# A one-layer hybrid encoder with 32 experts: the branch for crowded experts moved ahead of the last expert, and small loads put on shared semaphores

## The chip, the core and the metric

The kernel runs on one core of a Trainium2 chip. The time is that of one execution on the device in microseconds (us), as a median of several runs. The core has a matrix engine (TensorE, in the profile PE, its weight loads PEld), VectorE (DVE), ScalarE (ACT), GpSimd (POOL) and SyncE (SP). Each engine runs its own instruction stream in order, and the streams meet only at semaphores. Data moves between memory and the core by 16 DMA engines.

## What is computed

One layer on a sequence of 256 tokens of width 1024, all in float32. A mixing part (attention and a state-space branch) comes first. Then each token goes to its 4 best of 32 experts, and at the end an embedding term is added through a gate:

```
logits = hf @ w_router + b_router            # 256 x 32
top_val, top_idx = top_k(logits, 4);  gate = softmax(top_val)
# for every expert e, on the rows (tokens) that chose it:
gu  = xb @ w_up[e] + b_up[e]                  # 1024 -> 2048
g   = minimum(gu[:, :1024], 7);  up = clip(gu[:, 1024:], -7, 7)
act = (up + 1) * g * sigmoid(1.702 * g)
y   = act @ w_down[e] + b_down[e]             # 1024 -> 1024
x  += sum over the 4 experts of gate * y
# at the end
x  += sigmoid(rmsnorm(x, g_ple_gate) @ w_ple_gate) * rmsnorm(p @ w_ple_proj, g_ple_post)
```

An expert's weights are 12 MB (8 MB up, 4 MB down). Nothing bounds how many of the 256 tokens choose one expert. With these inputs no expert has over 64.

## The kernel before

**Pieces and ring.** An expert is six pieces of 2 MB: pieces 0 to 3 are the up weights, 4 and 5 the down weights. They go through a ring of 9 places in SBUF (`ring`). SP issues the loads (`load_pair`, `load_piece`, DMA at L410 and, in two halves, L477). Ahead of each it waits until the piece that lay in the place before has been read (`left`, L467 and L469): PE counts up a semaphore when it has read a piece (`READ`, `.then_inc`). Behind the pieces of the 32 experts come two pieces of the gate's weights (L503).

**One expert on PE.** `up` (L1638) waits for pieces 0 to 3 in turn and multiplies the tokens that chose the expert, at most `CAP` = 64 of them, by the up weights into banks `UG` and `UU`. `gather` (L1612) collects the next expert's tokens. `down` waits for the activation, transposes it (L1676), transposes the selection (L1680), multiplies by pieces 4 and 5 (L1694), adds the next expert's bias into `UG` and `UU` (`up_bias`, L1514), and scatters the result to the tokens (L1712). DVE clamps and multiplies (L1154 to L1162) and adds the scattered result to the residual (L1180). ACT does the sigmoid (L761) and two copies (L763, L765).

**Order of the experts.** PE has experts 0 to 2 and 27 to 31 written out, and those between in a loop of three experts a turn. ACT and DVE loop over one expert a turn. Within expert 12 the embedding product and the bias of the down product are done beside the rest (`embeddings`, L1739 and L1749, `bias_too`, L1710).

**The last expert** (31, `n == E - 1`) is written out apart on PE and DVE, in ACT it is the last turn of its loop. Its piece 3 and piece 5 come in two halves. PE turns the residual ahead (`turn_ahead`, L1653) into the banks `XT3B` and adds the last expert's share on top there (`scatter_turned`, L1662); DVE (L1170) and ACT (L782) copy the sum to `XT3`. Then come the gate's products (`gate`, L1817, 80 records), ACT's squares (L794), root (L796) and sigmoids (L800), DVE's products and sums (L813, L1259), and five stores by SP (L517).

**The branch for crowded experts.** DVE writes the largest count of tokens of an expert to `flag` early (`flag_set`). Each of PE, ACT, DVE and SP loads `flag` into a register (`value_load`) and, where it is over 64, runs loops over all experts and three further passes of 64 tokens each, on semaphores `M` that go on counting. This branch stands behind expert 31: on PE at L1790 between expert 31's scatter and the gate, on DVE at L1231, on ACT at L785, on SP at L507 behind the gate's loads. With these inputs it isn't taken, and each engine jumps over its body.

Of the kernel before, what the change touches and what calls it, by code (L numbers as in the profile page):

```python
# [68 lines left out]
def hybrid_layer(nc, x, p, g_mix, w_in, g_q, g_k, w_attn, a_re, a_im, log_dt, b_re, b_im, c_re, c_im, d_skip,  # L69
# [19 lines left out]
    with ExitStack() as ctx:  # L89
# [34 lines left out]
        def spread(ap, n):  # L124
# [47 lines left out]
                 for at in (6, 7)]  # L172
# [67 lines left out]
        names = ("x_in_0 x_in_1 half_in gain_mix_in params_in later_in dt_in bc_in ident_set odd_set b_zero x_sq x_ms x_root x_normal dt_rows angle_set "  # L240
                 "sine_set turn_set bbar_set pool_tables_set head_sq head_ms head_ms_all head_root heads_set "
                 "abs_set soft_set sp_set cum_full early_gates_set back_set gelu_set sz_set mixed_set x_again "
                 "x2_sq x2_ms x2_root x2_normal xn_set xn_half w_sum m_sum prod_full prod_read router_in router_set slots_set top_set exp_set chosen_set sel_first_set "
                 "gx_half xs_half cnt_full flag_set gates_ready "
                 "down_bias_in gain_in gate_gain_in cast_set cast_first_set rest_set_0 rest_set_1 up_bias_in up_bias_set post_in ple_in pp_ms pp_root "
                 "pt_full pt_set pp_full pp_set gt_full gt_set over_done late_0 late_1 late_2 xt3_late xt3_again xt3_read xt3_again_set x3_set x3_sq x3_ms x3_root xt3_full xt3_set pg_full "
# [3 lines left out]
                     "at_set y_full y_set sc_full sc_add dve_step").split()  # L250
        M = {n: sem("e_" + n) for n in moe_names}

# [12 lines left out]
        READ = {c: sem(f"read{c}") for c in (0, 1, 2, 4)} | {3: M["up_u"], 5: M["y_full"]}  # L265
# [30 lines left out]
        OVER = [spot(E - 1, c) for c in range(PER_EXPERT)]  # L296

# [94 lines left out]
        def _(sp):  # L392
# [20 lines left out]
            for key in W_ORDER:  # L413
# [14 lines left out]
                if key == ("attn", 0):  # L428

                    sp.dma_start(GFFN.rearrange("p (c k) -> p c k", k=4),  # L430
                                 g_ffn[0].rearrange("(c p k) -> p c k", p=P, k=4)).then_inc(S["gain_in"], 16)
                    sp.dma_start(GROUT.rearrange("p (c k) -> p c k", k=2),
                                 g_ffn[0].rearrange("(c p k) -> p c k", p=P, k=2)).then_inc(S["router_in"], 16)
                    sp.dma_start(WR.rearrange("p (c k) n -> p c k n", k=2),
                                 w_router[0].rearrange("(c p k) n -> p c k n", p=P, k=2)).then_inc(S["router_in"], 16)
                    sp.dma_start(BROUT, b_router[0:1, :].broadcast_to([P, E])).then_inc(S["router_in"], 16)
                    sp.dma_start(GPLE.rearrange("p (c k) -> p c k", k=4),
                                 g_ple_gate[0].rearrange("(c p k) -> p c k", p=P, k=4)).then_inc(S["gate_gain_in"], 16)
                if key == ("in", 1):

                    sp.wait_ge(S["b_zero"], 1)
# [56 lines left out]
            for n in range(LAST, E):  # L498
                for c in range(0, PER_EXPERT, 2):
                    load_pair(n, n, c)  # L500
            for c, at in enumerate(GATE_AT):
# [3 lines left out]
            sp.wait_ge(S["flag_set"], 1)  # L505
            crowd = sp.value_load(flag[0:1, 0:1], min_val=0, max_val=SEQ)
            with sp.If(crowd > CAP):  # L507
                sp.wait_ge(M["y_full"], E)
                with sp.Fori(0, E) as e:
                    with sp.Fori(0, PASSES) as j:  # L510
                        n = E + e * PASSES + j
                        for c in range(PER_EXPERT):
                            sp.wait_ge(READ[c], n)
                            load_rows(OVER[c], expert_source(e, c))
# [7 lines left out]
        def _(pool):  # L522
# [18 lines left out]
            pool.sem_inc(S["ident_set"], 1)  # L541
            pool.iota(ODD.bitcast(I32), [[0, 1]], base=0, channel_multiplier=1).then_inc(S["odd_set"], 1)
            pool.memset(area(A_GATE, 2 * TILES * 2 * GC), 0.0).then_inc(S["b_zero"], 1)
# [46 lines left out]
            for g in range(4):  # L590
                rows = slice(E * g, E * (g + 1))
                pool.dma_start(BDOWN[rows, :], b_down[0, :, 512 * (g % 2):512 * (g % 2 + 1)]).then_inc(S["down_bias_in"], 16)
            pool.dma_start(GPOST, g_ple_post[0:1, :].broadcast_to([P, D])).then_inc(S["post_in"], 16)
# [3 lines left out]
        def _(act):  # L597
# [6 lines left out]
            act.wait_ge(S["ident_set"], 1)  # L604
# [139 lines left out]
            def embeddings():  # L744
# [3 lines left out]
                act.wait_ge(S["gt_full"], 1)  # L748
                act.activation(GT, bank[ATB][:, 0:SEQ].rearrange("p (t n) -> p t n", t=TB),
                               ACT.Copy).then_inc(S["gt_set"], 1)  # L750
# [34 lines left out]
            with act.If(crowd > CAP):  # L785
                with act.Fori(0, E) as e:
                    with act.Fori(0, PASSES) as j:
                        expert(M, E + e * PASSES + j)
                act.wait_ge(S["over_done"], 1)


# [13 lines left out]
        def _(dve):  # L805
# [18 lines left out]
            dve.wait_ge(S["ident_set"], 1)  # L824
# [82 lines left out]
            dve.wait_ge(S["odd_set"], 1)  # L907
# [191 lines left out]
            dve.wait_ge(S["router_in"], 16 * 3)  # L1099
# [32 lines left out]
            dve.wait_ge(S["gain_in"], 16)  # L1132
# [52 lines left out]
            def expert(m, n, last=False):  # L1185
# [9 lines left out]
                else:  # L1195
                    dve.wait_ge(S["gate_gain_in"], 16)
# [25 lines left out]
            dve.wait_ge(S["post_in"], 16)  # L1222
# [7 lines left out]
            expert(M, E - 1, True)  # L1230
            with dve.If(crowd > CAP):  # L1231
                dve.wait_ge(M["pick_set"], E)
                dve.wait_ge(M["sc_add"], 4 * E)
                dve.wait_ge(S["xt3_late"], 2)
# [621 lines left out]
```

## Time and profile before

| | |
|---|---|
| median of 3 runs | 1182.69 us (1181.35 to 1182.91) |
| the profiled execution, its time | 1182.57 us |
| its span, first to last instruction | 1180.8 us |
| PE busy | 1122.5 us, 95% |
| DVE, ACT, POOL busy | 33%, 15%, 12% |
| DMA | 441 MB, 374 GB/s over the span |
| mean granted clock of TensorE | 0.994 of 2.4 GHz |

The profiled execution's time is 1.8 us above its span; what lies outside the span isn't in the trace. The profile's first part gives the busy time of each engine, the second the span in 40 equal slices of 29.5 us with busy shares in tenths. The chain follows the work that ended last back through what each step waited for. Matrix products in float32 show as more records than the program has products (L1638: 32 products an expert, 64 records).

### The profile page before, as it was taken

The numbers are of one execution on the slowest core, as the hardware profiler recorded it, in microseconds if no ns is written. First come the engines' busy times: TensorE is split into PE (matmuls) and PEld (weight loads), VectorE is DVE, ScalarE is ACT, GpSimd is POOL, SyncE is SP. The second block draws the span as 40 slices with busy tenths as digits, with TensorE's granted clock in tenths as the row PEclk, the third lists the DMA queues.
The fourth block names the chain that finished last, engine by engine and source line by source line (L and its number), as shares of the span: only waits on it lengthen the run. The fifth ranks groups of instructions, "written<-read, shape, count | busy, mean of one in ns | idle before, by whom it ended". The sixth has DMA issues, their size and how long they took to land.

```text
span 1180.8 us, 15718 instructions
## 1 busy us (share of the span) xinstructions
PE 1122.5 (95%) x6546; PEld 500.2 (42%) x6546; DVE 392.3 (33%) x840; ACT 173.4 (15%) x265; POOL 138.4 (12%) x163
## 2 busy tenths in 40 slices
PE   8999999999999999999999999999999998999988
PEld 4588887533333333333323333333333333333344
DVE  6547858442222232222222222322222232222222
ACT  2262012410000000000211111111111111111121
POOL 2995664300000000000000000000000000000000
PEclk9999999999999999999979999999999999999999
DMA  9931447799999999999999999999999999999980
GB/s 303 345 125 73 142 164 296 299 411 398 426 433 432 427 436 432 426 436 428 428 386 437 426 431 435 425 435 431 428 436 430 430 437 430 425 428 425 426 349 36
DMA packets 39482, 441.23 MB, mean 374 GB/s; under 512 B 9684, under 2 KB 10000, under 8 KB 22288
## 3 DMA queue, kind: packets, MB, share of 16 engines
q1 hardware_dynamic: 38224, 436.91, 88.2%
q0 software_dynamic: 1104, 3.67, 1.0%
q8 instruction: 34, 0.56, 0.2%
q14 instruction: 8, 0.07, 0.0%
q10 hardware_dynamic: 112, 0.02, 0.0%
HBM read 439.54 MB, written 1.05 MB: 373 GB/s over the span
## 4 chain that ended last, share of the span: by engine, by line
PE 81%; DMA 10%; DVE 6%; ACT 2%; issue 1%; POOL 0%; DVEq 0%; SPq 0%; ACTq 0%
PE bank L1638 33%; PE bank L1694 17%; DMA ring<-in_w_up_dram 9%; PE bank L1318 7%; PE bank L1712 5%; PE bank L1333 3%; PE bank L1817 2%; PE bank L1478 2%; PE bank L1514 2%; PE bank L1676 2%; DVE arena L1162 2%; DVE arena L1158 2%; DVE arena L1156 2%; PE bank L1486 1%; ACT arena L763 1%
## 5 line engine op out<-in xcount | busy, mean ns | idle before, releaser
L1638 PE MATMUL bank<-ring,arena 128*64 128x512 f32 x2048 | 450.5, 596 | 5.2 <-DMA ring<-in_w_up_dram 5.2
L1638 PEld LDWEIGHTS bank<-ring,arena 128*64 128x64 f32 x2048 | 143.7, 137 | 306.3 <-issue 294.1
L1694 PE MATMUL bank<-ring,arena 128*64 128x512 f32 x1024 | 227.0, 595 | 15.4 <-ACT arena L763 15.0
L1180 DVE TENSOR_TENSOR arena<-arena,bank 128x512 f32<-128x512 f32 x128 | 79.9, 683 | 293.6 <-PE bank L1712 293.4
L1154 DVE TENSOR_SCALAR arena<-bank 128x512 f32<-128x512 f32 x32 | 22.1, 692 | 345.6 <-PE bank L1638 345.6
L1694 PEld LDWEIGHTS bank<-ring,arena 128*64 128x64 f32 x1024 | 71.1, 137 | 150.6 <-issue 132.3
L761 ACT ACTIVATE arena<-arena 128x512 f32<-128x512 f32 x32 | 20.2, 631 | 467.7 <-DVE arena L1154 467.7
L1318 PE MATMUL bank<-arena,ring 128*128 128x256 f32 x384 | 86.4, 382 | 0.0
L1318 PEld LDWEIGHTS bank<-arena,ring 128*128 128x128 f32 x384 | 71.8, 190 | 12.7 <-issue 3.5
L1712 PE MATMUL bank<-arena 64*128 64x512 f32 x256 | 69.7, 627 | 0.0
L1612 PEld LDWEIGHTS bank<-arena 128*128 128x128 bf16 x1488 | 45.1, 98 | 25.2 <-issue 25.2
L765 ACT ACTIVATE arena<-bank 128x512 f32<-128x512 f32 x32 | 19.1, 597 | 231.1 <-PE bank L1694 231.1
L1612 PE MATMUL bank<-arena 128*128 128x64 bf16 x1488 | 48.8, 193 | 0.0
L1676 PE MATMUL bank<-ident,arena 128*128 128x128 f32 x128 | 23.8, 309 | 23.7 <-DVE arena L1162 23.7
L557 POOL TENSOR_TENSOR ring<-arena,ring 128x512 f32<-128x512 f32 x32 | 39.6, 1273 | 29.3 <-PE bank L1392 19.4
L1712 PEld LDWEIGHTS bank<-arena 64*128 64x128 f32 x256 | 23.6, 188 | 43.5 <-issue 43.5
L1333 PE MATMUL bank<-ring,arena 128*128 128x512 f32 x96 | 41.9, 595 | 0.0
L1514 PE MATMUL bank<-arena 32*64 32x512 f32 x256 | 34.8, 613 | 0.0
L763 ACT ACTIVATE arena<-bank 128x512 f32<-128x512 f32 x32 | 19.1, 597 | 79.6 <-PE bank L1676 79.6
L1676 PEld LDWEIGHTS bank<-ident,arena 128*128 128x128 f32 x128 | 17.8, 209 | 27.6 <-DVE arena L1162 25.7
L1817 PE MATMUL bank<-ring 128*128 128x512 f32 (+1 forms) x80 | 27.7, 508 | 1.5 <-issue 1.5
L1478 PE MATMUL bank<-arena,ring 128*128 128x256 f32 x128 | 27.8, 379 | 0.0
(263 smaller groups left out, 772.6 us busy)
## 6 DMA issues: line engine op xcount, KB each, us to landing
ring<-in_w_up_dram SPq DMA_DIRECT2D x42, 4096.0 KB, 23.7
ring<-in_w_down_dram SPq DMA_DIRECT2D x25, 4096.0 KB, 26.0
ring<-in_w_up_dram SPq DMA_DIRECT2D x42, 2048.0 KB, 26.1
ring<-in_w_down_dram SPq DMA_DIRECT2D x13, 2048.0 KB, 35.3
ring<-in_w_in_dram SPq DMA_DIRECT2D x7, 2048.0 KB, 16.8
ring<-in_w_glu_dram SPq DMA_DIRECT2D x2, 2048.0 KB, 8.2
ring<-in_w_out_dram SPq DMA_DIRECT2D x2, 2048.0 KB, 7.8
ring<-in_w_up_dram SPq DMA_DIRECT2D x4, 1024.0 KB, 36.3
```

Of the source, the lines that this page charges most:

```text
L557: pool.tensor_tensor(pairs(BACK[:, j, s, :]), pairs(ROT[:, i % 3, :]), table[:, i:i + 1, :].broadcast_to([P, 2, SEQ]), ALU.mult).then_inc( ...
L1180: dve.tensor_tensor(part, part, bank[at][:, :], ALU.add).then_inc(m["sc_add"], 1)
L1318: last = pe.matmul(b[:, SEQ * i:SEQ * (i + 1)], weight(key, a)[:, k, P * m:P * (m + 1)], rhs[:, k, :], start=(k == 0), stop=(k == n - 1))
L1333: last = pe.matmul(b[:, :], HT[:, k, t * P:(t + 1) * P], weight(("in", n), DT)[:, k, :], start=(k == 0), stop=(k == DT - 1))
L1478: last = pe.matmul(b[:, SEQ * h:SEQ * (h + 1)], weight(("glu", k // 2), 2)[:, k % 2, P * m:P * (m + 1)], GY[:, k, :], start=(k == 0), stop ...
L1514: pe.matmul(bank[UG + w][HALF * h:HALF * (h + 1), :], PICK[rows, :], BUP[rows, :], start=True, stop=False)
L1612: last = pe.matmul(bank[GX][:, CAP * d:CAP * (d + 1)], XB[t][:, part, P * d:P * (d + 1)], SELB[:, t, :], start=(i == 0), stop=(i == 3 * TB ...
L1638: last = pe.matmul(bank[UG + w][HALF * h:HALF * (h + 1), :].rearrange("p (m j) -> p m j", j=4), XS[:, k, :], columns[:, h, :, :], start=Fa ...
L1676: last = pe.transpose(bank[ATB][:, P * j:P * (j + 1)], rows[:, j, :], I)
L1694: last = pe.matmul(bank[YB][HALF * c:HALF * (c + 1), :], ACTT[:, j, HALF * h:HALF * (h + 1)], piece[:, j, 512 * c:512 * (c + 1)], start=(h ...
L1712: pe.matmul(bank[at][:, :], WSELT[rows, t, :], Y[rows, :], start=not bias_too, stop=True).then_inc(m["sc_full"], 1)
L1817: last = pe.matmul(bank[at][:, 0:cols.stop - cols.start], XT3[:, k, P * t:P * (t + 1)], WPG[k // (DT // 2)][:, k % (DT // 2), cols], start ...
```

## The change

The branch's body now stands ahead of expert 31 on all four engines, and it works on a set of semaphores of its own, `O` (for the ring's pieces one shared semaphore, `over_in`), that start at zero. On ACT expert 31 is therefore written out behind the loop, too. Since expert 31's bias already lies in `UG` and `UU` when the branch is reached, the body takes it out first (`drop_bias`) and puts it, with expert 31's tokens and selection, back at its end. The second turning of the residual that the old place needed is gone. On SP the body stands between the loads of expert 30 and those of expert 31; the gate's loads are behind expert 31's as before.

Beside that, small loads and settings share semaphores: `consts_set` for three constants of POOL, `gains_in` for five small loads of SP, `ple_in` for the seven of POOL, `pt_full` and `pt_set` for two steps each. Some waits therefore ask for more than before: the router's gain product on DVE waits for all five small loads, the embedding step on PE for all seven of POOL's. DVE drops two waits (`gain_in`, `gate_gain_in`). The semaphores that count read pieces belong to `M` now and are counted as before.

```diff
@@ SP
-            for n in range(LAST, E):
+            for n in range(LAST, E - 1):
                 for c in range(0, PER_EXPERT, 2):
                     load_pair(n, n, c)
+            sp.wait_ge(S["flag_set"], 1)
+            crowd = sp.value_load(flag[0:1, 0:1], min_val=0, max_val=SEQ)
+            with sp.If(crowd > CAP):
...
+            for c in range(0, PER_EXPERT, 2):
+                load_pair(E - 1, E - 1, c)
             for c, at in enumerate(GATE_AT):
...
-            sp.wait_ge(S["flag_set"], 1)
-            crowd = sp.value_load(flag[0:1, 0:1], min_val=0, max_val=SEQ)
-            with sp.If(crowd > CAP):
-                sp.wait_ge(M["y_full"], E)
...
@@ ACT
-            with act.Fori(ASIDE + 1, E) as e:
+            with act.Fori(ASIDE + 1, E - 1) as e:
                 expert(M, e)
             act.wait_ge(S["flag_set"], 1)
             crowd = act.value_load(flag[0:1, 0:1], min_val=0, max_val=SEQ)
-            act.wait_ge(S["gate_gain_in"], 16)
+            with act.If(crowd > CAP):
+                with act.Fori(0, E) as e:
+                    with act.Fori(0, PASSES) as j:
+                        expert(O, e * PASSES + j)
+            expert(M, E - 1)
+            act.wait_ge(S["gains_in"], 16 * 5)
@@ DVE
-            dve.wait_ge(S["router_in"], 16 * 3)
+            dve.wait_ge(S["gains_in"], 16 * 5)
             dve.tensor_tensor(WR, WR, spread(GROUT, E), ALU.mult).then_inc(S["router_set"], 1)
...
             crowd = dve.value_load(flag[0:1, 0:1], min_val=0, max_val=SEQ)
-            expert(M, E - 1, True)
             with dve.If(crowd > CAP):
...
+                select(O, E - 1, SLOT[:, 0:CAP])
+                pick(O, E - 1)
+                gathered(O, E * PASSES)
+            expert(M, E - 1, True)
@@ PE
             crowd = pe.value_load(flag[0:1, 0:1], min_val=0, max_val=SEQ)
+            with pe.If(crowd > CAP):
+                drop_bias()
+                pe.wait_ge(M["xs_set"], E)
+                with pe.Fori(0, E) as e:
+                    with pe.Fori(0, PASSES) as j:
...
+                gather(O, E * PASSES)
+                up_bias(O, E * PASSES)
+                pe.wait_ge(O["xs_set"], E * PASSES + 1)
+                pe.wait_ge(O["sc_add"], 4 * E * PASSES)
             up(M, E - 1, ring_piece(E - 1))
             pe.wait_ge(M["sc_add"], 4 * (E - 1))
             for i in range(3):
                 turn_ahead(i)
             down(M, E - 1, ring_piece(E - 1), bias_of_next=False)
-            with pe.If(crowd > CAP):
-                pe.wait_ge(S["xt3_set"], 2)
...
@@ embeddings, PE
-                    pe.wait_ge(S["ple_in"], 32)
+                    pe.wait_ge(S["ple_in"], 16 * 7)
```

On PE, before, between the scatter of expert 30 (L1712, first row) and the gate (L1817); L1784 is the load of `flag`, L1790 the branch, L1793 to L1653 below it its body:

```order
L1712 MATMUL bank<-arena 128x512 x4
L1784 TENSOR_LOAD flag
L1784 ISA x2
L1638 MATMUL bank<-ring,arena 64x512 x32
...
L1662 MATMUL bank<-arena 128x256 x8
L1712 MATMUL bank<-arena 128x512 x4
L1790 COMPARE_AND_BRANCH
L1793 UNCONDITIONAL_BRANCH
...
L1653 MATMUL bank<-ident,arena 128x128 x16
L1790 UNCONDITIONAL_BRANCH
L1817 MATMUL bank<-ring 128x512 x24
```

On PE, now, the same stretch (L1720 is the scatter, L1647 the up product, L1821 the gate):

```order
L1720 MATMUL bank<-arena 128x512 x4
L1789 TENSOR_LOAD flag
L1789 ISA x2
L1790 COMPARE_AND_BRANCH
L1522 MATMUL bank<-arena,neg_ones 64x512 x4
L1793 UNCONDITIONAL_BRANCH
...
L1790 UNCONDITIONAL_BRANCH
L1647 MATMUL bank<-ring,arena 64x512 x32
...
L1670 MATMUL bank<-arena 128x256 x8
L1720 MATMUL bank<-arena 128x512 x4
L1821 MATMUL bank<-ring 128x512 x24
```

The branch and its body moved from between the last scatter and the gate to between the load of `flag` and expert 31's up product; nothing stands between the last scatter and the gate.

On SP, now, between the loads of expert 30 and of expert 31 (L414 and L481 are the weight loads, L511 and L515 those of the body, L507 the branch):

```order
L414 DMA ring<-in_w_down_dram 128x4096 x2
L506 TENSOR_LOAD flag
L506 ISA x2
L507 COMPARE_AND_BRANCH
L511 DMA ring<-in_w_up_dram 128x4096 x4
...
L507 UNCONDITIONAL_BRANCH
L414 DMA ring<-in_w_up_dram 128x4096 x3
L481 DMA ring<-in_w_up_dram 128x2048 x2
```

Before, these rows stood behind the gate's two loads; the eight issues of expert 31 and the two of the gate are behind them now.

## Rows read from the trace of the kernel before

**Rows 1.** The page: the 40 slices of the span.

```profile
PEclk9999999999999999999979999999999999999999
DMA  9931447799999999999999999999999999999980
```

**Rows 2.** Windows, busy us of each engine, then PEclk, DMA share, GB/s.

```profile
976.00:1146.00 170.00, 156.98 (x952) 59.82 (x950) 40.33 (x80) 18.21 (x25) 0.00 (x0) 1.00 1.00 426
1146.00:1150.00 4.00, 2.52 (x10) 1.02 (x7) 2.72 (x6) 2.82 (x5) 0.00 (x0) 1.00 0.19 72
```

**Rows 3.** Chain that ended last, from 1080 us: start us, us, what.

```profile
1084.42 39.52 DMA ring<-in_w_up_dram
...
1123.98 7.23 PE bank L1638 x32
...
1142.01 0.61 ACT arena L765
...
1147.82 1.48 issue
1149.30 27.76 PE bank L1817 x80
```

**Rows 4.** Timeline of PE, experts 30 to 31: start, us, what [idle before].

```profile
1113.89 1.99 PE L1712 MATMUL bank<-arena 64*128 64x512 f32 x8
1115.81 7.09 PE L1638 MATMUL bank<-ring,arena 128*64 128x512 f32 x32
1123.98 7.21 PE L1638 MATMUL bank<-ring,arena 128*64 128x512 f32 x32 [1.09 <-DMA ring<-in_w_up_dram]
```

**Rows 5.** Timeline of ACT, the same stretch and the end.

```profile
1112.99 0.60 ACT L765 ACTIVATE arena<-bank 128x512 f32<-128x512 f32 x1 [7.77 <-PE bank L1694]
...
1131.11 0.63 ACT L761 ACTIVATE arena<-arena 128x512 f32<-128x512 f32 x1 [16.22 <-DVE arena L1154]
...
1146.14 0.84 ACT L782 ACTIVATE ring<-bank,small 128x256 f32<-128x256 f32 x2 [0.25 <-PE bank L1662]
...
1151.63 0.20 ACT L796 ACTIVATE small<-small 128x2 f32<-128x2 f32 x1
```

**Rows 6.** Timeline of DVE, the same stretch and the end.

```profile
1130.38 0.69 DVE L1154 TENSOR_SCALAR arena<-bank 128x512 f32<-128x512 f32 x1 [12.33 <-PE bank L1638]
```

**Rows 7.** Timeline of SP: issues of the last weight loads.

```profile
1065.63 3.76 SPq L410 DMA_DIRECT2D ring<-in_w_down_dram  x2
1073.65 11.09 SPq L410 DMA_DIRECT2D ring<-in_w_up_dram  x3
```

**Rows 8.** DMA issues: KB each, median us from issue to landing.

```profile
ring<-in_w_up_dram SPq DMA_DIRECT2D x4, 1024.0 KB, 36.3
ring<-in_w_ple_gate_dram SPq DMA_DIRECT2D x2, 2048.0 KB, 40.4
```

**Rows 9.** DMA queues of 1145 to 1149 us: packets, MB, share.

```profile
q8 instruction: 1, 0.02, 1.8%
```

**Rows 10.** One tile or line each: when it was loaded or used.

```profile
L437 SPq DMA_DIRECT2D small<-in_g_ple_gate_dram x1: 452/452/452, 60.3 to 60.3; - x1
...
L1100 DVE TENSOR_TENSOR router<-router,small x1: 418/418/418, 214.6 to 214.6; 128x256 f32<-128x256 f32 x1
...
L593 POOL DMA_DIRECT2D arena<-in_g_ple_post_dram x1: 560/560/560, 231.9 to 231.9; - x1
...
L1739 PE MATMUL bank<-ident,arena x4: 272/273/329, 567.8 to 568.2; 128*128 128x128 f32 x4
```

**Rows 11.** Timeline of PE around the half clock.

```profile
598.45 1.12 PE L1710 MATMUL bank<-arena 32*128 32x512 f32 x2
...
611.50 15.88 PE L1638 MATMUL bank<-ring,arena 128*64 128x512 f32 x64
```

**Rows 12.** The same windows view, of the half clock alone.

```profile
601.80:615.40 13.60, 13.60 (x20) 3.42 (x21) 4.83 (x8) 1.49 (x2) 0.00 (x0) 0.50 0.96 413
```

**Rows 13.** Waits of PE: us in total, times, longest us.

```profile
PE bank L1638 <- DMA ring<-in_w_up_dram: 5.2, 5, 1.7
```

More of the change, by code:

```diff
@@ L264, in hybrid_layer @@
         LAST_READ.update({("in", 4 + i): f"g{2 * i + 1}" for i in range(4)})
-        READ = {c: sem(f"read{c}") for c in (0, 1, 2, 4)} | {3: M["up_u"], 5: M["y_full"]}
+        LAST_OF = {0: "read0", 1: "read1", 2: "read2", 3: "up_u", 4: "read4", 5: "y_full"}
+        READ = {c: M[LAST_OF[c]] for c in range(PER_EXPERT)}
         def place(i, n=1):
@@ L497, in _ @@
                         load_pair(g * PERIOD + j, j, c)
-            for n in range(LAST, E):
+            for n in range(LAST, E - 1):
                 for c in range(0, PER_EXPERT, 2):
                     load_pair(n, n, c)
+            sp.wait_ge(S["flag_set"], 1)
+            crowd = sp.value_load(flag[0:1, 0:1], min_val=0, max_val=SEQ)
+            with sp.If(crowd > CAP):
+                for c in range(PER_EXPERT):
+                    left(E - 1, c)
+                for c in range(PER_EXPERT):
+                    sp.dma_start(place(OVER[c]), expert_source(0, c)).then_inc(over_in, 16)
+                with sp.Fori(1, E) as e:
+                    sp.wait_ge(O["y_full"], e * PASSES)
+                    for c in range(PER_EXPERT):
+                        sp.dma_start(place(OVER[c]), expert_source(e, c)).then_inc(over_in, 16)
+                sp.wait_ge(O["y_full"], E * PASSES)
+            for c in range(0, PER_EXPERT, 2):
+                load_pair(E - 1, E - 1, c)
             for c, at in enumerate(GATE_AT):
@@ L784, in _ @@
                 last.then_inc(S["xt3_late"], 1)
[L785 to L789, printed above, removed]
             for t in range(TB):
@@ L1514, in up_bias, with drop_bias @@
                         pe.matmul(bank[UG + w][HALF * h:HALF * (h + 1), :], PICK[rows, :], BUP[rows, :], start=True, stop=False)
+            def drop_bias():
+                for w in range(2):
+                    for h in range(2):
+                        rows = slice(E * (2 * w + h), E * (2 * w + h + 1))
+                        pe.matmul(bank[UG + w][HALF * h:HALF * (h + 1), :], neg_ones[rows, 0:CAP], BUP[rows, :],
+                                  start=False, stop=True)
             def gather_first(t, ds):
@@ L1642, in up, with turn_ahead @@
                     if c < 3:
-                        last.then_inc(READ[c], 1)
+                        last.then_inc(m[LAST_OF[c]], 1)
                     if beside is not None:
                         beside(c)
-            def turn_ahead(i, alone=False):
+            def turn_ahead(i):
                 for k in (2 * i, 2 * i + 1):
@@ L1652, in turn_ahead @@
                         at = SEQ * (k % 2) + P * t
-                        last = pe.matmul(bank[XT3B[i]][:, at:at + P], rows[:, t, k % 4, :], I,
-                                         start=(k % 2 == 0 and t == 0), stop=alone, is_transpose=True, skip_group_check=True)
-                return last
+                        pe.matmul(bank[XT3B[i]][:, at:at + P], rows[:, t, k % 4, :], I,
+                                         start=(k % 2 == 0 and t == 0), stop=False, is_transpose=True, skip_group_check=True)
             def scatter_turned():
@@ L1743, in embeddings @@
                         last = pe.transpose(bank[ATB][:, P * t:P * (t + 1)], GATES4[:, t, :], I)
-                    last.then_inc(S["gt_full"], 1)
+                    last.then_inc(S["pt_full"], 1)
                 elif c < 3:
@@ L1784, in _ @@
             crowd = pe.value_load(flag[0:1, 0:1], min_val=0, max_val=SEQ)
+            with pe.If(crowd > CAP):
[3 more added lines that the diff above has]
+                    with pe.Fori(0, PASSES) as j:
+                        n = e * PASSES + j
+                        gather(O, n)
+                        up_bias(O, n)
+                        here = over_piece(e)
+                        up(O, n, here)
+                        down(O, n, here, bias_of_next=False)
+                gather(O, E * PASSES)
+                up_bias(O, E * PASSES)
+                pe.wait_ge(O["xs_set"], E * PASSES + 1)
+                pe.wait_ge(O["sc_add"], 4 * E * PASSES)
             up(M, E - 1, ring_piece(E - 1))
@@ L1789, in _ @@
             down(M, E - 1, ring_piece(E - 1), bias_of_next=False)
-            with pe.If(crowd > CAP):
-                pe.wait_ge(S["xt3_set"], 2)
-                pe.wait_ge(S["xt3_late"], 2)
-                with pe.Fori(0, E) as e:
-                    with pe.Fori(0, PASSES) as j:
-                        n = E + e * PASSES + j
-                        gather(M, n)
-                        up_bias(M, n)
-                        here = over_piece(e * PASSES + j)
-                        up(M, n, here)
-                        down(M, n, here, bias_of_next=False)
-                pe.wait_ge(S["over_done"], 1)
-                for i in range(4):
-                    last = turn_ahead(i, True)
-                last.then_inc(S["xt3_again"], 1)
-                pe.wait_ge(S["xt3_again_set"], 1)
             def gate(part, ks):
```

92 lines of the change are left out of this document (39 added, 53 removed).

## The prediction

> **What bounds the kernel now.** I read the slices first, then the stretches at the end, then the chain. The slices show TensorE at full clock but for one stretch, and the DMA engines full from the tenth slice until the last but one [rows 1]. From 976 to 1146 us, experts 28 to 31, the DMA share is 1.00 at 426 GB/s [rows 2]. This is the stream of weights, and the chain says the same: from 1084.42 us on it is one DMA piece of 39.52 us, and it returns to PE only at 1123.98 us, when piece 2 of expert 31 has landed [rows 3]. The loads take 36 to 40 us from issue to landing there [rows 8], where a piece of 2 MB at 426 GB/s is worth 4.9, so some seven or eight pieces are always queued. After 1146 us the stream is over: 72 GB/s [rows 2]. So two clocks run one behind the other: the stream sets 1123.98 us, and what follows on PE (and, between its steps, on DVE and ACT) sets the rest, 56.8 us to the span's end at 1180.8.
>
> In that rest one piece is nobody's work: 1.48 us of "issue" from 1147.82 to 1149.30 us, between the last scatter and the gate's first product [rows 3]. What the gate waits for is done by then: ACT's last copy begins at 1146.14 and ends at 1146.98 [rows 5]. The gate's weights are the last pieces of the stream, which has run out by about 1146 us [rows 2]. What stands there in the program is the branch, not taken into its body but jumped across it. And in those 4 us one packet of 0.02 MB goes over the queue that is named instruction [rows 9]. I read the gap as PE fetching the code behind the jump.
>
> **Part 1, the tail of PE.** The jump leaves this place, so the gate follows the scatter at once: minus 1.5 us. Nothing else is late there. The copies are done at 1146.98. The reciprocal root that the first sigmoid needs hangs on DVE's and ACT's own steps, ready soon after 1151.8 [rows 5], while the first sigmoid comes after 24 of the gate's products, some 10 us past its start. Everything behind moves with PE.
>
> **Part 2, the same jump ahead of expert 31.** Now PE goes from the scatter of expert 30 to the load of `flag`, the branch, and across a body that is somewhat longer than the old one, to expert 31's up product. Today that product starts at 1115.81 us, right on the scatter [rows 4], with the load of `flag` hidden already; so the hole h is all new. The trace doesn't show it, but shows its twin. Low end: the same visible gap, 1.5 us. It would be lower only if the scatter covered more, and here it has 1.99 us of scatter behind the last wait [rows 4], in the tail 5.1 us of products (1142.7 to 1147.8). High end: no cover at all. In the tail, ACT's copy that releases the last products ends at 1142.61 and the gate begins at 1149.30 [rows 3], 6.7 us for dispatch, branch and fetch together. The same copy of expert 30 ends at 1113.59 [rows 5]; plus 6.7 is 1120.3, a hole of 4.5 us. The load of `flag` now stands ahead of the jump and might add a little; the fetch now runs beside a full weight stream, too. I take the middle, h = 3.0 us, since the cover here is smaller than the tail's but there is some.
>
> What hides it: PE waits 1.09 us for piece 2 at 1123.98 today, and the 32 records after it take 7.21 us where the 32 before took 7.09, so another 0.1 goes to a late half of piece 3 [rows 4]. A hole of up to 1.2 us thus costs nothing. What is above it comes out at the end in full, because behind piece 3 no step waits for a load [rows 3]. So plus 3.0 minus 1.2 is 1.8 us. By the low end it is 0.3, by the high end 3.3.
>
> **Part 3, SP.** The load of `flag` and the jump come between the issues of expert 30's down pieces and of expert 31's piece 0. The former end at 1069.39 us, the latter comes at 1073.65 after a wait for PE [rows 7]; 4.2 us lie free, nearly the 4.5 of the worst jump above. Were SP late by two or three us even so, seven pieces are queued and the DMA engines would not see it. Zero; without that queue it would cost its own length.
>
> **Part 4, DVE and ACT.** Both jump in an idle stretch: DVE's next work waits 12.33 us [rows 6], ACT's 16.22 us [rows 5]. Their old jumps lay beside the waits at the end. Zero on both sides.
>
> **Part 5, shared semaphores.** The router's product on DVE now waits for the gate's gains as well. They are issued at 60.3 us, the product runs at 214.6 [rows 10]. PE's embedding step at 567.8 waits for the last of POOL's loads too, issued at 231.9 [rows 10]. The three constants are set by one engine in order, so their counts mean what the single ones meant. Zero.
>
> **Sum.** Against the profiled execution's 1182.57 us: minus 1.5, plus 1.8, is **1182.9 us**. That execution lies 0.1 below the median of the three runs, so it stands for them. By the ends of h the sum is 1181.4 and 1184.4.
>
> **The rivals.** *The jump is nearly free when it comes early (chance 0.2).* Then h stays at or under 1.2, PE waits for piece 2 just as today, and the whole 1.5 us are gained: 1181.1 us. For it speaks that PE's queue has 1.99 us of scatter to work through. Against it: a gap of 1.48 us was left in the tail although 5.1 us of products stood ahead. The Trainium skill (Advanced Engine Details and Errata, Control Flow Timing) gives a compare-and-branch as some 108 ns, and by that alone this rival is the outcome. It has another page (Runtime: NRT & Kernel Launch, Instruction fetch mechanics) by which a taken branch to code that isn't loaded waits for a DMA fetch of the target; the 1.48 us and the instruction packet agree with this one, not with 108 ns.
>
> *The clock falls in the hole (chance 0.12); this ends slower.* TensorE's granted clock fell to its lower level, 1.2 GHz, once: at 601.8 us, after PE had been at the small products L1710 and L1712 since 598.45 and not idle at all [rows 11, 12]. It came back at 615.4, 3.9 us after the large products had begun at 611.50, and these 64 records took 15.88 us in place of twice 7.09: 1.7 us. The hole comes behind such small products (L1514, L1712). Longest wait for weights so far: 1.7 us, without a fall [rows 13]. If a hole of 4.5 us lets it fall, the time is 1184.4 plus 1.7, 1186.1 us; with a hole of 3.0 it is 1184.6. It decides from a hole clearly over 1.7 us on. Against it: the jump follows on two us of densely paired scatter products, and dense work resumes at once.
>
> *The gap in the tail isn't the jump's (0.07).* If it is PE's own start of the gate, it stays, and only the new hole counts: 1182.57 plus 0.3 to 3.3, about 1184.4 us. Against: no other change of product shows such a gap.
>
> *SP is late enough to let the queue run dry (0.03).* It needs a delay of some 30 us by the landing times [rows 8]; each us past that costs one. About 1187 us for a few.
>
> **How the numbers follow.** My forecast, a hole of 2 to 4.5 us, has 0.55; the rivals have 0.42, and 0.03 is for what I don't see. A measurement tells about 0.2% from no change, 2.4 us: faster means under 1180.3, slower over 1185.1. The forecast, the free jump and the gap that stays all lie inside, but for the scatter of runs (1.6 us between the three). Faster gets 0.05 (a part of the free jump with scatter), slower 0.12 (the fallen clock with a long hole, SP, a part of the scatter at the high end), the same 0.83. The range goes from the free jump less half a us of scatter, 1180.6, to the high end plus one, 1185.4; it leaves out the fallen clock behind a long hole.
>
> **What would show it.** In the changed profile: the piece "issue" between the last scatter and the gate gone, below 0.2 us; an idle of 2 to 4.5 us ahead of expert 31's first up product, put down to issue; PE's wait for piece 2 of expert 31 gone or under 0.5 us; an instruction packet near that hole; piece 2 landing within 1 us of 1124, DMA share 1.00 until 1146; the clock at full level from 1110 on. I'm wrong if the tail's gap stays, if the hole is under 1.2 us, if the clock falls, or if the weights land later than now.

## The result, and the profile after

The changed kernel takes **1187.23 us** (median of 7 runs, 1186.38 to 1190.49), the kernel before 1182.69 in the same session (7 runs, 1181.35 to 1184.72). The ratio is 1.0035, with a 95% interval of 1.0024 to 1.0047. It is 4.5 us slower, 0.35%; 1182.9 was forecast, and the range ended at 1185.4. The profiled execution took 1187.73 us with a span of 1186.0, against 1182.57 and 1180.8, so 5.2 us are there to be found. Some runs of every kernel, the one before too, take some 3 us longer, and the traces of experiments 1 and 7, taken in such runs, have one more stretch at half clock, at 228 us, behind which all comes some 2 us late.

The chain that ended last, of the changed kernel (start us, us, what), answers to [rows 3]:

```profile
1069.29 39.78 DMA ring<-in_w_down_dram
...
1113.78 1.92 PE bank L1720 x8
1115.70 5.31 issue
1121.01 16.89 PE bank L1647 x64
...
1152.56 1.95 PE bank L1720 x7
1154.51 27.72 PE bank L1821 x80
```

Two things are as foretold. The 1.48 us between the last scatter and the gate are gone: L1720 ends at 1154.51 and L1821 starts there. And there is a new hole ahead of expert 31's up product (L1647), put down to "issue". It is 5.31 us, though, and behind it the 64 records take 16.89 us. PE's timeline of the same stretch (start, us, what, idle before) answers to [rows 4]:

```profile
1113.71 1.99 PE L1720 MATMUL bank<-arena 64*128 64x512 f32 x8
1121.01 16.88 PE L1647 MATMUL bank<-ring,arena 128*64 128x512 f32 x64 [5.31 <-issue]
```

The wait for piece 2 is gone, as expected. Why the product is long shows in the windows view of the changed kernel (busy us of PE, PEld, DVE, ACT, POOL, then PEclk, DMA share, GB/s), which answers to [rows 12] and [rows 2]:

```profile
604.60:615.00 10.40, 10.40 (x19) 2.77 (x20) 4.38 (x8) 1.49 (x2) 0.00 (x0) 0.51 1.00 429
1115.70:1121.00 5.30, 0.00 (x0) 0.02 (x1) 2.17 (x5) 0.00 (x0) 0.00 (x0) 0.92 1.00 420
1121.00:1127.00 6.00, 5.99 (x16) 1.94 (x18) 0.00 (x0) 0.00 (x0) 0.00 (x0) 0.51 1.02 426
1127.00:1138.00 11.00, 11.00 (x53) 3.89 (x50) 0.77 (x2) 0.21 (x1) 0.00 (x0) 1.00 1.01 425
```

TensorE's granted clock is at its lower level, 1.2 GHz, from 1120.1 us, 0.9 us before the hole ends, until 1127 us. The stream of weights goes on untouched meanwhile, share 1.00. The slices of the page show the same second dip, which [rows 1] didn't have:

```profile
PEclk9999999999999999999989999999999999999899
DMA  9931447899999999999999999999999999999960
```

The other rows: SP's issues, the instruction packet (DMA queues of 1117 to 1121 us), and PE's waits of the changed kernel (us in total, times, longest), which answer to [rows 7], [rows 9] and [rows 13]:

```profile
1065.86 3.76 SPq L414 DMA_DIRECT2D ring<-in_w_down_dram  x2
1073.26 11.10 SPq L414 DMA_DIRECT2D ring<-in_w_up_dram  x3
```

```profile
q8 instruction: 1, 0.02, 1.7%
```

```profile
PE bank L1647 <- issue: 5.3, 1, 5.3
...
PE bank L1647 <- DMA ring<-in_w_up_dram: 4.3, 4, 2.3
```

The packet in the hole doesn't prove a fetch: experiment 2, without a hole, has one in the same stretch.

**The sum, closed.** The hole, 5.31. The clock, 16.89 less 13.97 (the same 64 records at full clock, in an experiment below): 2.92. Against it what the hole hid: the wait of 1.09 and the 0.35 by which 7.09 and 7.23 [rows 3, 4] exceed 13.97: 1.44. The tail's gap, 1.48. PE reached the place 0.11 earlier (1115.70 for 1115.81). 5.31 + 2.92 - 1.44 - 1.48 - 0.11 = 5.2 us, the difference of the spans.

### The profile page after: what moved, and what is told of

It is laid out like the page before. It is cut to its first block, busy times and chain, and to the rows that moved or that the text cites. A ratio compares the mean times of both kernels' runs of the same rounds, so it can differ in the third digit from the quotient of the medians.

```text
span 1186.0 us, 15711 instructions
## 1 busy us (share of the span) xinstructions
PE 1124.8 (95%) x6546; PEld 502.3 (42%) x6546; DVE 391.3 (33%) x840; ACT 172.1 (15%) x264; POOL 138.6 (12%) x163
## 4 chain that ended last, share of the span: by engine, by line
PE 81%; DMA 9%; DVE 5%; ACT 2%; issue 1%; POOL 1%; POOLq 0%; SPq 0%; DVEq 0%; ACTq 0%
PE bank L1647 34%; PE bank L1702 17%; PE bank L1319 7%; DMA ring<-in_w_down_dram 6%; PE bank L1720 5%; PE bank L1334 4%; DMA ring<-in_w_up_dram 3%; PE bank L1515 2%; PE bank L1821 2%; PE bank L1479 2%; PE bank L1684 2%; DVE arena L1163 2%; DVE arena L1167 2%; DVE arena L1161 2%; PE bank L1487 1%; ACT arena L771 1%
## 5 line engine op out<-in xcount | busy, mean ns | idle before, releaser
L1647 PE MATMUL bank<-ring,arena 128*64 128x512 f32 x2048 | 453.3, 599 | 9.6 <-issue 5.3
L1647 PEld LDWEIGHTS bank<-ring,arena 128*64 128x64 f32 x2048 | 145.1, 138 | 312.3 <-issue 303.5
L1720 PE MATMUL bank<-arena 64*128 64x512 f32 x256 | 68.8, 623 | 0.0
L1720 PEld LDWEIGHTS bank<-arena 64*128 64x128 f32 x256 | 23.5, 188 | 42.7 <-issue 42.7
L1334 PEld LDWEIGHTS bank<-ring,arena 128*128 128x128 f32 x96 | 18.6, 197 | 22.5 <-issue 22.4
```

The source lines that it names most:

```text
L1334: last = pe.matmul(b[:, :], HT[:, k, t * P:(t + 1) * P], weight(("in", n), DT)[:, k, :], start=(k == 0), stop=(k == DT - 1))
L1647: last = pe.matmul(bank[UG + w][HALF * h:HALF * (h + 1), :].rearrange("p (m j) -> p m j", j=4), XS[:, k, :], columns[:, h, :, :], start=Fa ...
L1720: pe.matmul(bank[at][:, :], WSELT[rows, t, :], Y[rows, :], start=not bias_too, stop=True).then_inc(m["sc_full"], 1)
```

## The experiments

Ten kernels ran, each beside the kernel before on the same chip. The medians of the kernel before were 1182.5 to 1182.7 us, and 1184.4 beside experiment 10. The gains of 1.1 to 1.4 us that experiments 1, 2, 7 and 9 show in their medians are clear of the interval of the ratio in experiment 1 alone, and just so; what follows is read from the traces. The spans of experiments 1 and 7 are not compared with the others', only what lies at the branch.

### 1. PE without the branch

```diff
@@ PE
-            crowd = pe.value_load(flag[0:1, 0:1], min_val=0, max_val=SEQ)
-            with pe.If(crowd > CAP):
-                drop_bias()
...
-                pe.wait_ge(O["sc_add"], 4 * E * PASSES)
             up(M, E - 1, ring_piece(E - 1))
```

> The changed kernel with PE's branch left out altogether (flag load, jump and body), all else as changed; a layer with over 64 tokens for one expert would not be computed. Theory A (the whole loss is PE's jump: a hole while the code behind it is fetched, and the fallen clock behind it): no hole ahead of expert 31, PE waits about 1 us for piece 2 again, no half clock there, no gap in the tail, 1181.2 us (1180.5 to 1182.2). Rival B (the jumps of SP, ACT or DVE, or the shared semaphores, carry part of the loss): the time stays at or above 1183, weights land later than in the kernel before or another engine's wait stands on the chain.

Measured: 1181.25 us (1180.05 to 1183.82, 10 runs), ratio 0.9989 [0.9979, 0.9998]. The chain of this kernel, around expert 31's second half, and at the gate:

```profile
1126.35 7.11 PE bank L1647 x32
...
1148.12 1.95 PE bank L1720 x7
1150.07 27.72 PE bank L1805 x80
```

The first 32 records follow the scatter at once, piece 2 is waited for again, and the gate follows its scatter. SP, ACT and DVE still branch, and all shared semaphores are in. So Parts 3, 4 and 5 cost nothing that can be measured, and all of the loss is PE's. Its clock stays at full level from 1118 to 1138 us. The rival of a late SP falls.

### 2. The branch stays, its body is short

```diff
             with pe.If(crowd > CAP):
                 drop_bias()
-                pe.wait_ge(M["xs_set"], E)
-                with pe.Fori(0, E) as e:
...
-                pe.wait_ge(O["sc_add"], 4 * E * PASSES)
+                gather(O, 0)
```

> The changed kernel, but the body of PE's branch cut to its first products and one gather (some 110 instructions in place of some 490), so that the jump ends in code that is next in line; flag load, branch and jump remain. The branch for crowded experts is not computed. Theory A (the hole is the fetch of code that is not loaded): no instruction packet at the hole, hole under 1.2 us, no fall of the clock, 1181.2 us (1180.5 to 1182.5). Rival C (the hole is flag load, compare and jump themselves, whatever the distance): hole 4 to 5.3 us, the clock may fall, 1185 to 1187.5.

Measured: 1181.45 us (1180.45 to 1184.72, 10 runs), ratio 0.9999 [0.9988, 1.0009]. The load of `flag`, the comparison and the jump are all still there; the jump goes over 52 products in place of 166. The chain of this kernel:

```profile
1084.85 39.45 DMA ring<-in_w_up_dram
...
1124.34 7.11 PE bank L1647 x32
...
1146.10 1.95 PE bank L1720 x7
1148.05 27.72 PE bank L1809 x80
```

No hole; the stream of weights sets the end again, as in [rows 3]. The span is 1179.5 us, 1.3 below before's: the tail's gap. Here the load, the comparison and the jump all fit beside the 1.99 us of scatter ahead of them. What costs is the body: what is jumped over, and so where the jump lands.

One thing that was expected didn't come: there is an instruction packet all the same. The DMA queues of 1117 to 1121 us, of this kernel:

```profile
q8 instruction: 1, 0.02, 1.7%
```

What differs is the number. The queues of 1110 to 1135 us, of the changed kernel and then of this one:

```profile
q8 instruction: 3, 0.05, 0.8%
```

```profile
q8 instruction: 1, 0.02, 0.3%
```

In the same stretch experiment 1 has one packet, 3 and 4 have three, and 10 has two. More of them thus come with the far jump. That agrees with a fetch of the code behind the jump; no row shows PE waiting for a packet, so that this fetch is the hole is inferred.

### 3. `flag` loaded early

```diff
@@ PE, behind expert 0's up product
             pe.wait_ge(S["flag_set"], 1)
+            crowd = pe.value_load(flag[0:1, 0:1], min_val=0, max_val=SEQ)
             down(M, 0, ring_piece(0))
@@ PE, ahead of the branch
-            crowd = pe.value_load(flag[0:1, 0:1], min_val=0, max_val=SEQ)
             with pe.If(crowd > CAP):
```

> The changed kernel, with PE's load of the flag moved up to expert 0; branch and body stay where they are. This prices the flag load. In theory A the fetch makes up most of the hole: it shrinks from 5.3 us by 0.3 to 1.5 us to about 4.3, the clock may or may not still fall: 1184 to 1186.5. If the flag load is the bulk of it (rival C), the hole shrinks to under 2 us, the clock stays and the time is 1181.5 to 1182.5.

Measured: 1185.85 us (1185.41 to 1189.83, 5 runs), ratio 1.0040 [1.0021, 1.0059]. The chain of this kernel, and its windows:

```profile
1116.19 4.12 issue
1120.31 15.66 PE bank L1647 x64
```

```profile
1121.40:1124.60 3.20, 3.20 (x10) 1.02 (x8) 0.00 (x0) 0.00 (x0) 0.00 (x0) 0.50 0.99 410
```

The hole is 1.2 us shorter: that much of the 5.31 is the load of `flag`, standing in series with the rest, 4.12. The clock falls for a shorter while and costs 15.66 less 13.97, 1.7 us. The ratio, 1.0040 for 1.0035, doesn't tell this kernel from the changed one; the span is 1.9 us shorter.

### 4. The hole filled with products

```diff
             crowd = pe.value_load(flag[0:1, 0:1], min_val=0, max_val=SEQ)
+            pe.wait_ge(M["xs_set"], E)
+            for _ in range(6):
+                pe.matmul(bank[GX][:, :].rearrange("p (k n) -> p k n", k=DT), I, XS, start=True, stop=True)
             with pe.If(crowd > CAP):
```

> The changed kernel, with six more float32 products of 128x512 (unused results in a free bank, some 5.2 us of full array work) on PE ahead of the flag load and the jump. They delay expert 31 by about as much as the hole does, but PE is not idle. Theory A: the hole is covered to under 0.5 us, expert 31 starts near 1121 us as in the changed kernel, the clock does not fall, and the time is that of the changed kernel less the 3.0 us that the half clock costs: about 1184.2 us (1183.3 to 1185). Rival D (the clock falls for the small products ahead, not for the idle hole; or the hole comes behind the added products in full): the clock falls all the same and the time is 1187 or more; with an uncovered hole, 1190.

Measured: 1185.86 us (1185.14 to 1188.18, 8 runs), ratio 1.0027 [1.0015, 1.0039]; span 1183.6. The chain of this kernel, and its windows:

```profile
1115.98 5.35 PE bank L1791 x12
1121.33 0.22 issue
1121.55 13.97 PE bank L1647 x64
```

```profile
1115.70:1121.00 5.30, 5.30 (x14) 2.20 (x12) 2.45 (x6) 0.00 (x0) 0.00 (x0) 1.00 0.98 413
1121.40:1124.60 3.20, 3.05 (x15) 1.28 (x17) 0.00 (x0) 0.00 (x0) 0.00 (x0) 1.00 1.00 415
```

PE is as late as in the changed kernel (5.57 us for 5.31), but not idle, and the clock stays. The same 64 records now take 13.97 us, where they took 16.89, and the span is 2.4 us shorter. This shows that idleness of the hole made the clock fall, and its price. The time missed its expected range (1183.3 to 1185): the median is only 1.4 us below the changed kernel's, a us less than the spans say.

It shows one more thing. The six products take 5.35 us, and of the hole of 5.31 us 0.22 is left. So work that PE has queued ahead of the branch runs inside the stall, nearly us for us.

### 5 and 6. The branch at expert 24, with and without the early load

The whole function is kept: the branch stands behind expert 23 on all four engines, and experts 24 to 26 are written out on PE and SP. The kernel before still has waits for weights behind that place (here PE's timeline of before, from 905 us; start, us, what, idle before), the next in [rows 4] among them:

```profile
981.05 7.09 PE L1638 MATMUL bank<-ring,arena 128*64 128x512 f32 x32 [1.69 <-DMA ring<-in_w_up_dram]
...
1010.20 7.09 PE L1638 MATMUL bank<-ring,arena 128*64 128x512 f32 x32 [1.26 <-DMA ring<-in_w_up_dram]
```

They add up to 5.5 us with the smaller ones (0.93, 0.18, 0.36, 1.09), and so might swallow the hole.

```diff
@@ PE
-            with pe.Fori((ASIDE - FIRST) // PERIOD + 1, (LAST - FIRST) // PERIOD) as g:
+            with pe.Fori((ASIDE - FIRST) // PERIOD + 1, (MID - FIRST) // PERIOD) as g:
                 period(g)
-            for n in range(LAST, E - 1):
...
             with pe.If(crowd > CAP):
...
+            period((MID - FIRST) // PERIOD)
+            for n in range(LAST, E - 1):
...
```

> Full function. The changed kernel with the branch of all four engines ahead of expert 24 instead of expert 31, and PE's flag load moved up to expert 0. Theory A (the hole and the slow clock are PE time, and PE time is free as long as PE still waits for weights behind it): hole of about 4.1 us near 917 us, the clock may fall for some 7 to 10 us (2 to 3 us more); the waits for weights of experts 26 to 31, 5.6 us in the kernel before, shrink to about 0; piece 2 of expert 31 lands near 1124 us as before, the tail's gap is gone: 1181.4 us (1180.6 to 1182.8). Rival E (PE's late release of ring places starves the stream of weights there): the GB/s drops in that slice and every us of hole comes out at the end, 1185 to 1188.

> The same as e5_branch_at_24_flag_early, but with PE's flag load right ahead of the branch, as in the changed kernel. Theory A: hole 5.3 us, with the clock's share 7.3 to 8.3 us against 5.6 us of waits that can take it up: 1.7 to 2.7 us come out, less 1.5 of the tail: 1183.4 us (1182.3 to 1184.5). Rival E: 1186 or more.

Measured: with the early load 1182.52 us (1181.07 to 1185.66, 12 runs), ratio 0.9999 [0.9988, 1.0010]; without it 1182.79 (1181.90 to 1185.99, 10 runs), ratio 1.0007 [0.9997, 1.0016]. PE's timeline of the first of them, and then of the second:

```profile
915.66 1.99 PE L1725 MATMUL bank<-arena 64*128 64x512 f32 x8
922.27 16.23 PE L1652 MATMUL bank<-ring,arena 128*64 128x512 f32 x64 [4.62 <-issue]
```

```profile
923.30 15.56 PE L1652 MATMUL bank<-ring,arena 128*64 128x512 f32 x64 [5.79 <-issue]
```

The load of `flag` lengthens the hole by 1.2 us here, too, though the times can't be told apart. The fall of the clock comes as well: 16.23 and 15.56 less 13.95 (the same records at full clock, experiment 8). Of the 6.9 us of experiment 5 (4.62 and 2.28) most is swallowed, since the kernel is as fast as before; but the 1.5 us of the tail's gap, gained as well, are spent again. Both times lie in their expected ranges, but by luck: piece 2 of expert 31 was to land near 1124 us, and PE takes it up at 1125.95 and 1125.79 us, after waits of 1.09 and 0.69. Rival E, by which every us of the hole comes out, falls.

### 7. The kernel before, its body short

```diff
@@ PE, kernel before
             with pe.If(crowd > CAP):
                 pe.wait_ge(S["xt3_set"], 2)
...
+                gather(M, E)
```

> The kernel before, its branch at the old place behind expert 31, with the body of PE's branch cut to one gather (some 100 instructions in place of some 390); the branch for crowded experts is not computed. Theory A (the 1.48 us ahead of the gate are the fetch of code that is not loaded): gap under 0.2 us, no instruction packet there, 1181.2 us (1180.5 to 1182.2). Rival F (the gap is the compare and jump, or the gate's own start): gap 1.0 to 1.5 us, 1182.7.

Measured: 1181.41 us (1180.71 to 1184.73, 10 runs), ratio 0.9993 [0.9984, 1.0002]. The chain of this kernel at the place of the tail's gap:

```profile
1148.61 1.95 PE bank L1712 x7
1150.56 27.72 PE bank L1804 x80
```

No gap, with the branch where it was. The 1.48 us of [rows 3] were the jump's, and mostly hidden; the rival by which they were PE's own start of the gate falls. An instruction packet stands here as well, against what was expected: the queues of 1140 to 1152 us show one, where the kernel before has two.

### 8 and 9. What is left of the loss at expert 24

Both are experiment 5 with one edit: five products without use ahead of PE's branch, or PE's branch and its load of `flag` taken out.

```diff
+            pe.wait_ge(M["xs_set"], MID + 1)
+            for _ in range(5):
+                pe.matmul(bank[GX][:, :].rearrange("p (k n) -> p k n", k=DT), I, XS, start=True, stop=True)
             with pe.If(crowd > CAP):
```

> The branch at expert 24 with its count read before, and five products of 128x512 in float32 without use ahead of the branch on PE. The whole function is computed. Theory (what is left of the loss at 24 is PE's hole and the fall of the clock behind it): the products and what is left of the hole take about 4.6 us of PE, less than the 5.6 us that PE waited for weights behind the start of expert 24 in the kernel before; the clock stays at its full level behind them; 1181.3 us, about 1.2 below the kernel before. Rival (the stream of weights itself loses some 1.3 us when the branch stands there, wherever PE is): about 1182.5 us, as without the products.

> As the branch at expert 24, but PE has neither its branch nor the read of the count (no expert here has over 64 tokens); the other engines branch there. Theory (PE's lateness is what came out): no hole on PE, the waits for weights are back as before, 1181.2 us, since the gap at the tail is gone too. Rival (the branch of the queue that issues the weights, at expert 24, costs the stream): 1182.5 us with no hole on PE.

Measured: filled, 1184.79 us (1181.68 to 1187.02, 11 runs), ratio 1.0009 [0.9994, 1.0024], profiled run 1182.72 with a span of 1181.0. Without PE's branch 1181.50 (1180.39 to 1185.17, 11 runs), ratio 0.9990 [0.9978, 1.0003], span 1179.5. PE's timeline of the filled kernel, at expert 24 and at expert 31:

```profile
915.51 1.99 PE L1725 MATMUL bank<-arena 64*128 64x512 f32 x8
917.43 4.56 PE L1793 MATMUL bank<-arena,ident 128*128 128x512 f32 x10
922.08 13.95 PE L1652 MATMUL bank<-ring,arena 128*64 128x512 f32 x64
...
1111.06 3.65 PE L1707 MATMUL bank<-ring,arena 128*64 128x512 f32 x16 [1.36 <-DMA ring<-in_w_down_dram]
...
1117.58 7.09 PE L1652 MATMUL bank<-ring,arena 128*64 128x512 f32 x32
1125.77 7.09 PE L1652 MATMUL bank<-ring,arena 128*64 128x512 f32 x32 [1.10 <-DMA ring<-in_w_up_dram]
```

And that of the kernel without PE's branch:

```profile
1109.60 3.65 PE L1707 MATMUL bank<-ring,arena 128*64 128x512 f32 x16 [0.32 <-DMA ring<-in_w_down_dram]
...
1116.12 7.09 PE L1652 MATMUL bank<-ring,arena 128*64 128x512 f32 x32
1124.29 7.09 PE L1652 MATMUL bank<-ring,arena 128*64 128x512 f32 x32 [1.08 <-DMA ring<-in_w_up_dram]
```

The first theory missed for the filled kernel (1184.79 us in the median and 1182.72 in the profiled run, for 1181.3) and held for the other. The first product behind the branch comes 6.57 us after the scatter begins (922.08 less 915.51), and it was 6.61 without the added products (experiment 5: 922.27 less 915.66). So 4.56 us of products ahead of the branch ran wholly inside the stall.

The clock stays and only 4.65 us of PE go, yet piece 2 of expert 31 lands 1.5 us later (1125.77 for 1124.29), and PE waits for it as long as ever. The branches of the other engines are not to blame, since without PE's the loss is gone. A lateness of PE at expert 24 thus makes weights land late at expert 31. It isn't in proportion: piece 2 is taken up at 1125.77 to 1125.95 us in experiments 5, 6 and 8, whether PE was late by 4.65 us or by 6.9. PE frees the places of the ring, so SP issues behind it: the load at 989.28 us in the kernel without PE's branch comes at 991.24 in the filled one. The time that PE waits for weights was not all free for PE to be late in. How that lateness reaches piece 2 is open: by 1074 us SP is only 0.4 us behind, the DMA engines are full in both, and the bytes moved from 900 to 1120 us are the same within 0.1 MB, worth 0.2 us.

### 10. A body with the gathers in loops

```diff
             def gather(m, n):
...
+                looped = DT - 1 if m is O else 0
+                if looped:
+                    pe.matmul(bank[GX][:, 0:CAP], XB[0][:, 0, 0:P], SELB[:, 0, :], start=True, stop=True)
+                    with pe.Fori(0, looped) as d:
+                        for i in range(3 * TB):
...
-                for d in range(DT):
+                for d in range(looped, DT):
```

> The change as it is, the whole function, but the two gathers in PE's branch body are loops over seven of the eight pieces of a row: the body has 96 products where it had 166 (52 in the run with the short body, which had no hole). Theory (a jump costs nothing while its target lies in code that has been fetched already, and the first product behind it comes late once it lies beyond): somewhere between 52 and 166 products lies the point; if 96 lie inside, no hole, no fall of the clock, 1181.4 us, below both kernels; if not, the hole is what it was, 5.3 us, and 1186 to 1187 us. Rival (the hole grows with the length of the body, as if each instruction jumped over cost something): a hole of (96-52)/(166-52) of 5.3 us, about 2.0 us, of which 1.2 hide behind the wait for the second piece, and 1182.2 us.

Measured: 1187.22 us (1185.59 to 1190.44, 12 runs), before 1184.41 (17 runs), ratio 1.0027 [1.0014, 1.0041]. The chain of this kernel:

```profile
1116.01 4.88 issue
1120.90 15.66 PE bank L1655 x64
```

96 products are still too many, and the hole is 4.88 us where 5.31 went with 166. It doesn't grow in proportion to what is jumped over; it is there or it isn't, and if length decides, the point lies between 52 and 96 products. One rival wasn't tried: all bodies that stalled hold the loops over experts and passes, and the two that didn't (experiments 2 and 7) hold none. A body without loops but over 96 products long would tell length from loops.

## Why the prediction was wrong

**The mechanism was right, the size of h was not.** Part 2 named the step: a jump over the body, all of it new, what is above the cover coming out in full. It put h at 3.0 us, as the middle between a visible gap of 1.5 and 4.5 "with no cover at all". Measured: 5.31, above the high end. Two things were wrong in it.

First, the cover was taken off twice. The 4.5 comes from the 6.7 us that pass in the tail from ACT's copy to the gate. Counted from the same copy of expert 30, they hold the 1.99 us of scatter; 4.5 is what is left behind the scatter when it hides as much of the stall as it can. It is the value with full cover, and not with none, and nothing was left to subtract. Experiments 4 and 8 show that work ahead of the branch does run inside the stall. The copy of expert 30 in experiment 3, which has no load of `flag` there:

```profile
1113.30 0.60 ACT L773 ACTIVATE arena<-bank 128x512 f32<-128x512 f32 x1 [8.10 <-PE bank L1702]
```

From its end at 1113.90 to the first product at 1120.31 it is 6.4 us for 6.7, and 4.12 for 4.5 behind the scatter. The low end of 1.5 us had the tail's 5.1 us of products inside it, and these don't stand here.

Second, the load of `flag` was passed over with "might add a little"; it adds 1.2 us (5.31 less 4.12, and 5.79 less 4.62), in series. With 5.31 for 3.0 the sum moves from 1182.9 to 1185.2, at the edge of the range.

**The clock fell**, the rival that was given 0.12. Its place in the sum was nothing, and it measured 2.92 us. Between two products of PE the trace of before has no idle stretch longer than 1.7 us, for the 3.0 forecast, so the low chance had nothing under it. Later traces stay at full clock behind waits of 2.3 and 2.5 us and fall with every hole of 4.1 us and more; what one of 3.0 does wasn't seen. The argument against it, that dense work stands on either side, is worth nothing: so does it here. Its price was taken from the dip at 602 us as 1.7; it came out as 1.6 to 2.9 in the five kernels, in no order with the length of the hole. With h put right and the clock, the sum is 1188.1, and the profiled run took 1187.73.

**Near by luck.** The time nearest to the 1187.2 measured is the late SP's, 1187, whose mechanism didn't occur. The fallen clock behind a long hole, the right mechanism, had 1186.1, with both its terms too small.

**Right:** Part 1, the tail's gap is the jump's and goes with it: minus 1.48 for 1.5, shown by experiment 7. The cover of 1.2 us was 1.44. Part 3: SP isn't late; its first issue behind the branch is at 1073.26 us, 1073.65 before. Parts 4 and 5: zero, by experiment 1. The rule of the Trainium skill that was set against the trace (Runtime: NRT & Kernel Launch, Instruction fetch mechanics), that a taken branch to code that isn't loaded waits for its fetch, agrees with the runs: no hole over 52 products, one of 4.88 and 5.31 us over 96 and 166; no run shows the wait for the fetch by itself. The other page's 108 ns (Advanced Engine Details and Errata, Control Flow Timing) is no contradiction in this kernel: with a target close by (experiment 2) the branch cost nothing to be seen, and with a far one 4.1 us.

**Slips.** From 976 to 1146 us experts 26 to 31 run, and not 28 to 31; nothing hangs on it. The instruction packet that was read as the fetch of the gate's code is no sign of it taken alone: experiment 7 has one without the gap.

**The range** left out the fallen clock behind a long hole as one of two unlikely things. The two aren't independent: the clock fell in all five kernels with a long hole that was left idle.

## What to carry to other kernels

A branch that is hardly ever taken cost nothing here with a short body, and 4 to 6 us of its engine with a long one: put it where work stands queued ahead of it, keep its body short on the engine that sets the time, and load its condition long before. Price such a stall from where the engine is released, and take off the work that stands between that point and the branch, once. Add what the clock of TensorE loses behind it. Idle time of the engine that frees a ring's places may not be free: in experiments 5, 6 and 8 a part of what was spent there came back as later loads.

## What the runs showed of the hardware

A jump over 166 products left PE idle for 4.1 us behind a scatter of 2 us (4.6 at another place), over 96 about as much (4.88 with the load of a register, worth 1.2), and over 52 nothing. From the beginning of the scatter to the first product behind the jump it was 6.1 and 6.6 us, and 4.56 us of products put between left it at 6.6. Loading a register from SBUF on PE took 1.2 us in series with the stall, twice, and nothing to be seen without one. Instruction packets of 0.02 MB are more frequent around the far jump (three for one from 1110 to 1135 us); the DMA engines are full of weights meanwhile, and a stall with free DMA engines wasn't tried. TensorE's clock fell to half level in or just behind holes of 4.1, 4.6, 4.9, 5.3 and 5.8 us, for 3.4 or 6.8 us, and didn't behind waits of up to 2.5 us (the longest in experiment 9); products without use in the hole kept it up.

No run here took the branch, since no expert has over 64 tokens; what it costs then wasn't measured. No version that computes the whole function beat the kernel before. The experiments point to one, a body of at most some 50 products on PE; by experiment 2 it would take about 1181.4 us, 1.2 less, an estimate within the noise of one comparison. It wasn't written.
